# Tile 1's first two weight chunks after the last expert row, and tile 0's two gates of the odd layer beside tile 1's projections

## The reference

```python
def peer_ffn(h, w_query, sub_keys, peer_u, peer_v):
...
        u_sel = peer_u[idx]
        act = jax.nn.gelu(jnp.einsum('chkd,cd->chk', u_sel, hc).astype(jnp.float32),
                          approximate=False) * g
        v_sel = peer_v[idx]
        return jnp.einsum('chk,chkd->cd', act.astype(hc.dtype), v_sel)
```

## Time and profile before

| | |
|---|---|
| median of 3 runs | 1218.93 us (1217.1 to 1220.67) |
| the profiled execution | 1214.53 us, of which the span is 1212.9 |
| PE busy | 1041.7 us, 86% |
| DVE, ACT, POOL busy | 63%, 43%, 25% |
| moved by DMA | 395.21 MB, of which expert rows 270.91 |
| weight chunks | 2048 KB each (one of the odd layer 1120 KB) |
| constants after the experts | 1024, 128, 120, 64 and 16 KB |
| experts of tile 1, with tile 0's second block beside them | about 592 to 953 us |
| tile 1's even layer, with the rest of tile 0 | 953 to about 1100 us |
| tile 1's odd layer | to the end |

### The profile page before, as it was taken

The page is one execution under the profiler, slowest core; times in us unless marked ns, Lnnn a source line. Parts: engine busy times, 40 slices in busy tenths (PEclk is TensorE's granted clock), DMA queues, the critical chain, the costliest instruction groups (busy, mean ns, idle before and its releaser), DMA issues.

```text
span 1212.9 us, 11894 instructions
## 1 busy us (share of the span) xinstructions
PE 1041.7 (86%) x3616; PEld 530.2 (44%) x3616; DVE 765.1 (63%) x2013; ACT 525.0 (43%) x1367; POOL 308.3 (25%) x297
## 2 busy tenths in 40 slices
PE   4988887898888799886898978799798798899998
PEld 4755553433334344332344443344343344454564
DVE  5864645689998675568766777786666443242354
ACT  5331139834434534344645563455574213211332
POOL 0000112443445353335332323334234000000000
PEclk9998999999999989999898988999899899999999
DMA  8042798799999999999999999999999574437630
GB/s 315 12 163 79 299 403 328 268 414 414 360 403 374 426 421 424 423 423 420 406 428 426 424 422 367 411 426 419 425 422 421 204 277 156 200 148 277 235 150 18
DMA packets 51727, 395.21 MB, mean 326 GB/s; under 512 B 5536, under 2 KB 10400, under 8 KB 11472
## 3 DMA queue, kind: packets, MB, share of 16 engines
q0 software_dynamic: 37536, 270.91, 54.8%
q1 hardware_dynamic: 13552, 122.83, 25.2%
q10 hardware_dynamic: 576, 0.72, 0.2%
HBM read 393.38 MB, written 1.05 MB: 325 GB/s over the span
## 4 chain that ended last, share of the span: by engine, by line
PE 36%; DMA 19%; DVE 14%; ACT 6%; issue 3%; POOL 0%; DVEq 0%; ACTq 0%; POOLq 0%
DMA expert_rows<-in_peer_uv,peer_idx 18%; PE bank L1783 15%; PE bank L1445 11%; DVE expert_rows L1390 6%; PE bank L2015 2%; PE bank L2056 2%; PE bank L1654 1%; PE bank L1690 1%; PE bank L2031 1%; DVE r L973 1%; ACT L1513 1%; PE bank L1157 1%; ACT L1424 1%; ACT peer_diag L1431 1%; ACT peer_dots L1425 1%
## 5 line engine op out<-in xcount | busy, mean ns | idle before, releaser
L1445 PE MATMUL bank<-expert_rows,peer_diag 128*128 128x512 f32 x896 | 450.9, 637 | 96.4 <-ACT peer_diag L1431 96.2
L1458 POOL DMA_INDIRECT expert_rows<-in_peer_uv,peer_idx x256 | 296.1, 1157 | 531.9 <-PE bank L1445 436.6
L1390 DVE CUSTOM_DVE_ANT_0 expert_rows<-expert_rows,HN 128x1024 f32<-128x1024 f32 x256 | 309.8, 1221 | 123.9 <-DMA expert_rows<-in_peer_uv,peer_idx 122.7
L1445 PEld LDWEIGHTS bank<-expert_rows,peer_diag 128*128 128x128 f32 x896 | 169.9, 200 | 320.2 <-issue 165.3
L1783 PE MATMUL bank<-w_ring,b_xt 128*128 128x512 f32 (+1 forms) x576 | 275.7, 603 | 9.2 <-ACT b_sq L1814 4.4
L1424 ACT ACTIVATE peer_dots<-peer_dots 128x1 f32<-128x1 f32 x256 | 51.7, 202 | 332.1 <-DVE peer_dots L1390 331.3
L1783 PEld LDWEIGHTS bank<-w_ring,b_xt 128*128 128x128 f32 x576 | 105.5, 196 | 114.7 <-issue 107.0
L1431 ACT ACTIVATE peer_diag<-ident,peer_dots 128x128 f32<-128x128 f32 x224 | 89.9, 401 | 7.3
L1425 ACT ACTIVATE peer_dots<-peer_dots,peer_ex 128x1 f32<-128x1 f32 x256 | 75.4, 295 | 8.3
L1513 ACT ACT_TABLE_LOAD x53 | 68.0, 1283 | 18.6 <-DMA x_res<-in_x 5.6
L1424 ACT ACT_TABLE_LOAD x48 | 61.6, 1283 | 14.2 <-DVE peer_dots L1390 13.4
(11 more groups left out here) (389 smaller groups left out, 1141.0 us busy)
## 6 DMA issues: line engine op xcount, KB each, us to landing
w_ring<-in_w_in_e SPq DMA_DIRECT2D x16, 2048.0 KB, 11.5
w_ring<-in_w_in_o SPq DMA_DIRECT2D x14, 2048.0 KB, 11.4
w_ring<-in_w_query SPq DMA_DIRECT2D x8, 2048.0 KB, 10.1
w_ring<-in_w_out SPq DMA_DIRECT2D x4, 2048.0 KB, 8.6
w_ring<-in_w_out_e SPq DMA_DIRECT2D x4, 2048.0 KB, 11.0
w_ring<-in_w_out_o SPq DMA_DIRECT2D x4, 2048.0 KB, 7.3
w_ring<-in_w_in SPq DMA_DIRECT2D x2, 2048.0 KB, 15.6
expert_rows<-in_peer_uv,peer_idx POOLq DMA_INDIRECT x256, 12.3
```

The lines of the kernel that those rows point to most:

```text
L1390: t.dve.tensor_tensor_reduce(u, u, t.HN[:, it // PH, :], 1.0, 0.0, ALU.mult, ALU.add, self.dots[:, it, k:k + 1]).then_inc(*self.dotted.add())
L1445: ins = t.pe.matmul(t.PS[2 * T + c][:, :], self.diag[:, d % self.RD, :], self.slot(n)[:, D + c * 512:D + (c + 1) * 512], start=k == 0, sto ...
L1458: t.pool.indirect_dma_start(self.slot(n), None, t.dram["peer_uv"], bass.IndirectOffsetOnAxis(ap=self.idx[:, it, k:k + 1], axis=0)).then_in ...
```

## The change

Tile 1's first two chunks are no longer asked for in the loop over the experts. Behind the loop SP waits for the rows of the last expert but one (`arrived(NI * TOPK - 2)`, 255th of 256), and then asks for both, ahead of the five constants. In tile 0's odd layer `project` now gets `late = 6`: at job 6 it sets `"held"` and goes on only when `"far"` is set, that is, behind the experts. Jobs 6 and 7 (the gates) then use one bank instead of two in turn, and the form with exp and ln that tile 1 uses. What waited for `"asked"` after the loop waits for `"held"`.

```diff
+LATE = 6
...
-def project(L, matrix, jobs):
+def project(L, matrix, jobs, late=None):
...
+    soft = [T == 0 and (late is None or j < late) for j in range(len(plan))]
...
+    where = [j % nb if late is None or j < late else 0 for j in range(len(plan))]
+    prior = [max([i for i in range(j) if where[i] == where[j]], default=None) for j in range(len(plan))]
     for j, e in enumerate(emptied):
-        L.free[j % nb] = e
+        L.free[where[j]] = e
 
     def pe():
         for j, (c, n, kind, _, _, _) in enumerate(plan):
+            if j == late:
+                L.done["held"] = True
+                while "far" not in L.done:
+                    yield
             while not t.w.ready(T, matrix, c):
                 yield
             i = t.w.take(T, matrix, c, n)
             if j == 0:
                 t.pe.wait_ge(*L.done["xt"])
             t.w.wait(t.pe, i)
-            pa, free = banks[j % nb], emptied[j - nb] if j >= nb else before.get(j % nb)
+            pa, free = banks[where[j]], emptied[prior[j]] if prior[j] is not None else before.get(where[j])
...
-            elif kind == "gate" and T == 0:
+            elif kind == "gate" and soft[j]:
...
-    yield from woven(L, one_by_one(lambda: and_beside(L, asked(L, project(L, m, jobs)), turn_half(L, t.PS)),
+    yield from woven(L, one_by_one(lambda: and_beside(L, asked(L, project(L, m, jobs, (LATE, None)[T])), turn_half(L, t.PS)),
...
-        if n > 140 and "asked" in lanes[0].done and len(then) and t.w.open():
-            t.w.ahead(1, *then.pop(0))
+    t.sp.wait_ge(*peer.arrived(peer.NI * TOPK - 2))
+    while then and t.w.open():
+        t.w.ahead(1, *then.pop(0))
     for engine in (t.pe, t.dve, t.act, t.sp, t.pool):
         engine.wait_ge(*peer.total.at(2 * QT))
...
-    while "asked" not in lanes[0].done:
+    while "held" not in lanes[0].done:
         next(ahead)
```

More of the change, by code:

```diff
@@ L1799, in act @@
                 yield
-            ps = banks[j % nb]
+            ps = banks[where[j]]
             if j == 0:
@@ L1827, in act @@
                 sig = L.sig[:, :, :].rearrange("p h c -> p (h c)")
-                (logs if T else gelus)(t)
-                how = (ACT.Exp, minus) if T else (ACT.Tanh, half)
+                (gelus if soft[j] else logs)(t)
+                how = (ACT.Tanh, half) if soft[j] else (ACT.Exp, minus)
                 t.act.activation(sig, ps[:, 256:280], how[0], scale=how[1]).then_inc(*taken.add())
@@ L1843, in act @@
                 t.act.activation(L.rs[:, m, sl], L.hs[:, m, sl], ACT.Exp, scale=-0.5).then_inc(*rooted.add())
-            elif kind == "gate" and T:
+            elif kind == "gate" and not soft[j]:
                 yield
@@ L1859, in dve @@
                 t.dve.wait_ge(*summed.at(j + 1))
-                t.dve.tensor_tensor(x, banks[j % nb][:, 0:n], x, ALU.add).then_inc(*shut.add())
+                t.dve.tensor_tensor(x, banks[where[j]][:, 0:n], x, ALU.add).then_inc(*shut.add())
                 L.done["x"] = L.done["x", c // 512] = shut.at(j + 1)
@@ L1895, in dve @@
                 sig = L.sig[:, :, :]
-                if T == 0:
+                if soft[j]:
                     t.dve.tensor_scalar(sig, sig, 1.0, 0.5, ALU.add, ALU.mult).then_inc(*sigged.add())
```

## The result

The kernel after took 1253.4 us (median of 4, 1252.66 to 1255.62), against 1218.01 of the kernel before beside it (1214.43 to 1220.67): a ratio of 1.028 [1.024, 1.031]. The forecast was 1234 (1211 to 1245): the sign was right, the size was not, and the time lies above the range. The profiled execution took 1255.62 us, span 1253.8, so in the profiles the change costs 40.9 us of span where the sum said 15. By the medians it costs 35.4 us: the profiled execution before was close to the fastest of its kernel and the one after was the slowest of its own, so some 5 of the 40.9 us are the spread between executions.

The account below looks back on a forecast made before the run. DMA bytes were taken to bound the expert stage and PE's program order the stage behind it. The terms summed to +19.0 us, less 4 for overlap +15, giving 1234 us on the median; range 1211 to 1245.

Parts of the forecast that it names:

- part one: Expert stage: four weight chunks leave it and their bytes come back as time, -19.9 us (-16 to -19.9).
- a bound of 4 us: Expert stage: PE, ACT and the chain behind each row must keep a shorter period, so up to 4 us less gain.
- rival 2: Expert stage does not give its time back: the chain behind each row sets the period, +25 us, 1244; chance 0.11.
- Part two: Behind the experts: the two gates' matmuls move to a stage that PE bounds and cost in full, +13.9 us.
- Part three: Right after the experts: PE waits for gate 0's weight between the halves of tile 1's transposes, +13 us (+10.5 to +14).
- Part four: Behind the experts: loads wait for the three-slot weight ring: +3.2 for gate 1, +6.7 for `phi`, -3.4 for `w_out_o`.
- second term: At `Squeeze(1)`: the `phi` weight must wait for tile 1's chunk 1 to free its slot, +6.7 us (+4 to +8).
- The wait for `w_out_o`: Later behind the experts: PE's wait for `w_out_o`'s second chunk goes, as tile 0 runs five steps later, -3.4 us.
- Part five: Behind the experts: PE's granted clock drops after the new waits, +5.5 us (0 to +8).

Follow-up runs that it names:

- no_split: Kernel before, without the early multiplication of the first half of tile 1's even-layer output with `w_out_e`; all of it done at the end: 1.010 [1.006, 1.014].
- loads_cut: Kernel before with the four weight chunks (tile 0's two gates, tile 1's first two) fetching an eighth of their bytes, every instruction in place: 0.996 [0.993, 0.998].
- steps_held: Kernel before without tile 1's chunks in the loop and with no tile 0 step from expert 233 on: one execution, 1232.65 us beside 1218.14.
- gates_short: Kernel after with two of the eight matmuls of each late gate, the other steps empty: 1.024 [1.020, 1.029] of the kernel before.
- gates_moved: Kernel after with tile 1's first two chunks asked for in the loop as before, only the gates held: 1.032 [1.028, 1.036] of the kernel before.
- gate_first: Kernel after with gate 0's chunk asked for ahead of tile 1's two chunks: 1.017 [1.014, 1.020] of the kernel before.

## Why the prediction was off

**Its sum against the profiles.** It said +15 and the span says +40.9. Of the 25.9 between them, 11.7 are part one (-8.2 for -19.9), 12.1 the dropped half, 1.5 from ahead of the stage and 1.5 from behind the even layer, and -0.9 come from parts two to five: the stretch from the first transposes to the odd layer's grew by 46.1 us (145.4 to 191.5), less 12.1 is 34.0, where the parts gave 34.9. The 12.1 depends on where the place is cut (13.7 from SP's issue of `w_out_e`'s second chunk on, at 1077.83 and 1103.50); `no_split` confirms it by 11.7 in time, and by 12.5 at the same place of its profile. Two terms of about 12 us each failed; with one of them right and the other wrong, the forecast of 1234 would have been 1246, at the upper edge of the range.

**Part one failed, at the step "it counts in full if the gathers stay dense, which the three stretches say".** The first two stretches of the earlier trace rows have no chunk in flight, but the gathers in them stood behind a queue that the chunks had made: gathers took 17.0 us to land, against 8.4 once the chunks were gone. At 2.5 us of bytes a row, 17 us are some six or seven rows waiting, and a stretch of 8 or 10 us behind a chunk lives on that. The third stretch, 915 to 945, is dense for another reason: it has none of tile 0's steps, as the prediction says itself, and the kernel after is dense there too (1.01 at 920 to 940). What came back, by the stage's length, from what was taken out: seven eighths of the bytes of all four chunks 4.9 us (`loads_cut`), the four chunks and the gates' steps together 8 to 11 (after and the four kernels like it, 373.7 to 376.0), three of the chunks and all of tile 0's steps from expert 233 on 13.9 (`steps_held`). ACT at 9.98 of 10.5 and PE at 10.5 of 10.5 did say so. The prediction read them as a bound of 4 us instead of 12. Its own test for rival 2, a DMA share below 1 between 840 and 930, came true; the rival was right in its place and in its size (it priced itself at +10; it cost 11.7) and was given 0.11. Its cause was not right: `steps_held` has the chain dot, gelu, diagonal, matmul as it was, and there the DMA engines stay full; it is tile 0's steps between the experts that hold the chain up. The time that it gives, 1244, was not reached either, since it lacks the dropped half.

**Part two held** within what `gates_short` can tell, and the step that it rests on, that PE's idle pieces don't take the work in, is shown by the unchanged waits.

**Part three held.** Counted from the end of the add, the gate chunk was reckoned at 13.7 us and PE went on at 13.5; the second transposes ended 15.2 us later than before against 13 and 0.9 of gate work. Tile 0's first step did stand between the halves of the transposes. The Trainium skill's rule on ring order ("DMA: Bandwidth & Descriptors", "Queues, rings and completion order") agrees with this trace: the three chunks landed one after another, at 947.2, about 952.5 and 960.3, and the gate chunk, the last of them and behind the constants, took 11.1 us from its issue, where in `gates_moved`, with the constants alone ahead of it, it took 8.1. Put first in the ring (`gate_first`) it was there when PE came. The Trainium skill's advice on the same page, "Rules for kernel authors" (issue early, wait late), agrees as well: with the gate chunk issued 12 us earlier, its wait of 12.68 us was gone.

**Part four held but for its second term, which was too small.** Gate 1 waited 3.75 us for 3.2 predicted. The second term had 6.7 us, at most 8, for the `phi` weight alone. The program takes tile 1's third chunk into the ring ahead of it: PE waits 6.58 us for that chunk and then 2.86 for `phi`, issued 0.4 us behind it and landed after 11.9 us instead of 7.3 to 8.3. That is 9.4 together. The wait for `w_out_o` went, as predicted.

**Part five held roughly.** Behind the first wait PE did 2.93 and 4.50 us of work at 0.50, so 3.7 us were lost where 2.5 was allowed; behind the second the clock was 0.68 in one piece of 5 us with 3.22 of work, 1.0 lost where 3 was allowed; behind the third it was 0.50, 0.50 and 0.75 with 2.08, 2.73 and 5.00 of work, 3.7 lost for 3.4. The sum is near, the single sizes are not. One more such piece came with the dropped half, inside its 12.1 us.

**The term that was missing.** The prediction reckoned that tile 0 runs five steps later against tile 1 and followed that to the ring alone. The same shift also decides a condition in the program's writer, `"finished" in L.other.done`. No row of the trace before shows that condition; it shows its product, L1654 in front of L1690. Asking of each such line what it depends on would have found it. With part one at its measured size and this term the sum is 15 + 11.7 + 12.1 = +39, 1258 on the median of before and 1253 on its profiled execution, where 1253.4 and 1255.6 were measured: on the medians it is now 4 to 5 us too high, about the spread between executions.

## What to carry to other kernels

A stretch in which an extra transfer is absent and the DMA engines are still full proves nothing while a backlog drains: look at how long a transfer takes from issue to landing beside its own bytes, and at how full the other engines are, before counting bytes as time. Work moved off the shared stage lands whole in one that an in-order engine bounds, and its weight should be the first in the ring if its first use is the first thing behind. Where programs are merged step by step, list the decisions that the writer takes by how far the other program has come, since a shift of a few steps can switch one. And a remedy tried alone can move the same decision: look in its rows for what else came back before its gain is put down to one wait.

## What the runs showed of the hardware

A queue of gathers kept the sixteen engines at 1.00 to 1.01 through 8.5 and 10.5 us stretches although, with the chunks' bytes gone, the share falls to 0.93 and 0.78 (`loads_cut`, 870 to 900 and 900 to 920) or 0.88 and 0.92 (after). After PE stood still for 12.68 us its granted clock was 0.50 up to 970, ten us after its work began again, and 0.87 in the next five; behind the 3.4 us wait of the kernel before it was 0.57 and 0.75. Profiles of one program differ by 1 us in the expert stage, those with nearly the same program behind it by up to 6 us there, so a term of 3 us there has to be read from its own rows or from repeated timing.
